# Ninety-six rows in place of 128 in the expert passes of a hybrid decoder trunk

## The chip, the core and the metric

The kernel runs on one core of a Trainium2 chip. The metric is the device time of one execution in microseconds (us). PE is the tensor engine, PEld its loads of the stationary operand, DVE, ACT and POOL are the vector, scalar and general engines, SP issues DMAs.

## What is computed

A trunk of two layers over 256 tokens of width 1024, in fp32. Each layer is a mixer (attention, short convolution, gated linear attention) and then a channel mixer: dense SwiGLU in layer 0, eight experts of which each token uses two in layer 1. The second is what the change is about:

```python
D_MODEL, SEQ, N_EXPERTS, TOP_K, D_FF_EXPERT = 1024, 256, 8, 2, 3584

def swiglu(h, wg, wu, wd):
    return (jax.nn.silu(h @ wg) * (h @ wu)) @ wd

def moe_swiglu(h, router, eg, eu, ed):
    b, s, d = h.shape
    t = h.reshape(b * s, d)
    logits = (t @ router).astype(jnp.float32)
    top_v, top_i = lax.top_k(logits, TOP_K)
    top_w = jax.nn.softmax(top_v, axis=-1)
    combine = jnp.sum(jax.nn.one_hot(top_i, N_EXPERTS, dtype=jnp.float32) * top_w[..., None], axis=1)
    out = jnp.zeros((b * s, d), jnp.float32)
    for e in range(N_EXPERTS):
        out = out + combine[:, e:e + 1] * swiglu(t, eg[e], eu[e], ed[e]).astype(jnp.float32)
    return out.astype(h.dtype).reshape(b, s, d)
```

With the inputs of the reference its router gives the eight experts 58, 51, 66, 62, 68, 69, 59 and 79 tokens (512 in all).

## The kernel before

**Precision.** Every product is made of three matmuls in fp32r (`PASSES`): high part by high part, low part of the activations by high part of the weights, high part of the activations by low part of the weights.

**Weights as a stream.** All weights come as 400 units of 128x2048 fp32 (1 MB each). SP loads them in order into six buffers `raw` (`load_unit`, L312; it waits until DVE is done with the unit six before). ACT rounds a unit into its high part `w_hi` (`hi_unit`, L327), DVE subtracts that from `raw` and so gets the low part `w_lo` (`lo_unit`, L332), PE uses both. There are three buffers of each part (`SPLIT`), so ACT waits until PE is done with the unit three before (`unit_used`). A unit feeds 12 matmuls with 512 moving columns.

**One expert.** An expert works on up to 128 of its tokens, gathered as the columns of `xT_hi` and `xT_lo`. Its 3584 hidden columns are cut into 14 blocks of 256, of three units each: two for gate and up (`gate_up`, 24 matmuls, L1828) and one for down (`down`, `down_tile`, 12 matmuls, L1852). The tokens are always the stationary operand, 128 columns wide, and the weights move past them. Between gate_up and down of a block ACT takes silu (`gate_x`, L663), DVE multiplies (`act_x`, L1141), PE transposes the block by two transposes (`act_T`, L1844), ACT copies these out as `aT_hi` (L520) and DVE subtracts to get `aT_lo` (L1167). Blocks go in pairs (`expert`): transposes of the last pair, 48 matmuls of gate_up for the next pair, 24 of down for the last. The code is written out by hand for each engine; the order on each is fixed, and semaphores join them.

**Between experts.** POOL gathers the next expert's tokens from HBM with an indirect DMA into `small`, PE transposes them with eight transposes (`gather_T`, L1977), and ACT and DVE make the two parts (`gather_hi` L520, `gather_lo` L1196). An expert's output `y_sb` goes to `outs` in HBM and is added in four pieces in the last expert (`combine`, L1184). The first expert's tokens come by matmuls (`first_tokens`, L1807).

**Too many tokens.** While the first expert runs, DVE finds out which experts have over 128 tokens (`weights` sets `flag`, `crowded` counts and lists them, L1348 to L1355), between two units of the stream. If there are any, a general loop after the end (up to three laps) runs each of these experts again on its remaining tokens. Without them the loop is skipped.

Of the kernel before, what the change touches and what calls it, by code (L numbers as in the profile page):

```python
# [16 lines left out]
F32 = mybir.dt.float32  # L17
F32R = mybir.dt.float32r
I32 = mybir.dt.int32
# [26 lines left out]
FB = 256  # L46

# [33 lines left out]
ROWS = N_EXP * P  # L81
NO_ROW = (N_EXP - 1) * P
# [37 lines left out]
def build(nc, x, stream, w_z, w_gate, conv_w, gla_gain, gains, router, gain_t, consts, masks, out):  # L120
    with ExitStack() as ctx:
# [53 lines left out]
        zero8 = sb("zero8", [P, 8])  # L175
        over_f = sb("over_f", [P, 4])
        over_i = sb("over_i", [P, 4], I32)
# [75 lines left out]
        flag = small[:, 124:132]  # L253
        cum = small[:, 132:140]
        sel = small[:, 140:148]
# [94 lines left out]
        def _(sp):  # L350
# [26 lines left out]
            n_over = sp.value_load(over_i[0:1, 0:1], min_val=0, max_val=3)  # L377
# [14 lines left out]
            with sp.If(n_over > 0):  # L392
                with sp.Fori(0, n_over) as k:
                    e = sp.value_load(over_i[0:1, bass.ds(k + 1, 1)], min_val=0, max_val=N_EXP - 1)
# [16 lines left out]
        def _(pool):  # L411
# [8 lines left out]
            nc.gpsimd.memset(zero8[:, :], 0.0)  # L420
# [60 lines left out]
            pool.dma_start(outs[NO_ROW:ROWS, :], nothing).then_inc(none_out, 16)  # L481
            def gather(e):

                pool.wait_ge(id_cp, e)
                if e == 1:
                    pool.wait_ge(tok_out, 16 * TT)
                else:
                    pool.wait_ge(gaT_ps, 2 * e)
                pool.indirect_dma_start(small[:, D:2 * D], None, tokens[:, :],
                                        bass.IndirectOffsetOnAxis(ap=tok_i[:, e:e + 1], axis=0)).then_inc(ga_in, 16)  # L490

            for e in range(N_EXP - 1):
                gather(e + 1)
                pool.wait_ge(y_done, e + 1)
                pool.dma_start(outs[e * P:(e + 1) * P, :], y_sb).then_inc(y_out, 16)
# [14 lines left out]
        def _(act):  # L510
# [144 lines left out]
            def ffn_block(S, tiles, B, par, n, d=0):  # L655

                for t in range(tiles):
# [5 lines left out]
                    nc.scalar.activation(gate_x[:, s, :], ps[:, 4 + s, 0:FB], ACT.Silu,  # L663
# [15 lines left out]
            def ffn_aT(S, tiles, B, par):  # L679
# [4 lines left out]
                else:  # L684
                    copy(aT_hi[:, par, :, :], ps[:, 6 + par, 0:FB].rearrange("p (f q) -> p f q", f=2)).then_inc(S.aT_hi, 1)

            def gathered(k):

                act.wait_ge(ga_ps, k + 1)
                copy(gath[:, 0, :], ps[:, 2, :]).then_inc(ga_act, 1)  # L690

            def gather_hi(e, q, bank=2):

                for g in range(2):
                    act.wait_ge(gaT_ps, e * 2 + (g + 1))
                    copy(xT_hi[:, 4 * g:4 * g + 4, q * P:(q + 1) * P],
                         ps[:, bank + g, :].rearrange("p (k s) -> p k s", k=4)).then_inc(ga_hi, 1)

            def y_copy(e, n, d):
# [4 lines left out]
                copy(y_sb, ps[:, 0:2, :].rearrange("p a d -> p (a d)")).then_inc(y_done, 1)  # L704

            def expert_out(k, n, d):
# [3 lines left out]
                copy(ys_hi[:, :], ps[:, 0:2, :].rearrange("p a d -> p (a d)"), w_slot[:, 0:1]).then_inc(y_hi, 1)  # L710
# [97 lines left out]
            n_over = act.value_load(over_i[0:1, 0:1], min_val=0, max_val=3)  # L808
# [3 lines left out]
            copy(ys_hi[:, 0:512], ps[:, 0, :], w_slot[:, 0:1]).then_inc(end_hi, 1)  # L812
            used(act, ALL_UNITS)
            copy(ys_hi[:, 512:D], ps[:, 1, :], w_slot[:, 0:1]).then_inc(y_hi, 1)
# [26 lines left out]
        def _(dve):  # L841
# [291 lines left out]
            def ffn_block(S, tiles, B, par, n, d=0):  # L1133

                for t in range(tiles):
# [4 lines left out]
                    else:  # L1140
                        nc.vector.tensor_tensor(act_x[:, s, :], gate_x[:, s, :], ps[:, 4 + s, FB:2 * FB], ALU.mult).then_inc(S.mul, 1)  # L1141
# [16 lines left out]
            def ffn_aT(S, tiles, B, par):  # L1158
# [5 lines left out]
                else:  # L1164
                    dst, hi = aT_lo[:, par, :, :], aT_hi[:, par, :, :]
                    src = ps[:, 6 + par, 0:FB].rearrange("p (f q) -> p f q", f=2)
                nc.vector.tensor_tensor(dst, src, hi.bitcast(F32), ALU.subtract).then_inc(S.aT_lo, 1)  # L1167

            def dispatch(e, over):

                for t in range(TT):
                    s = slot[:, t, e:e + 1] if isinstance(e, int) else slot[:, t, bass.ds(e, 1)]
                    ins = nc.vector.tensor_scalar(disp[:, t, :], iota, 128.0 if over else 0.0, s, ALU.add, ALU.is_equal)
# [13 lines left out]
            def gathered(k):  # L1187

                dve.wait_ge(ga_ps, k + 1)
                nc.vector.tensor_copy(gath[:, 1, :], ps[:, 3, :]).then_inc(ga_dve, 1)  # L1190

            def gather_lo(e, q, halves=(0, 1), bank=2):

                for g in halves:
                    dve.wait_ge(ga_hi, e * 2 + (g + 1))
                    nc.vector.tensor_tensor(xT_lo[:, 4 * g:4 * g + 4, q * P:(q + 1) * P],  # L1196
                                            ps[:, bank + g, :].rearrange("p (k s) -> p k s", k=4),
                                            xT_hi[:, 4 * g:4 * g + 4, q * P:(q + 1) * P].bitcast(F32),
# [11 lines left out]
            def expert_out(k):  # L1210

                dve.wait_ge(y_hi, k + 2)
                nc.vector.scalar_tensor_tensor(out=ys_lo[:, :], in0=ps[:, 0:2, :].rearrange("p a d -> p (a d)"),
                                               scalar=w_slot[:, 0:1], in1=ys_hi[:, :].bitcast(F32), op0=ALU.mult,
# [115 lines left out]
            def weights():  # L1330

                dve.wait_ge(total_ps, 1)
                nc.vector.tensor_scalar(flag[:, :], ps[:, 7, 16:24], float(P), None, ALU.is_gt)
# [12 lines left out]
            def crowded():  # L1346

                link(nc.vector.tensor_tensor_scan(cum[:, :], flag[:, :], zero8[:, :], 0.0, ALU.add, ALU.add))  # L1348
                link(nc.vector.tensor_copy(over_f[:, 0:1], cum[:, 7:8]))
                for k in range(3):  # L1350
                    link(nc.vector.scalar_tensor_tensor(out=sel[:, :], in0=cum[:, :], scalar=float(k + 1), in1=flag[:, :],
                                                        op0=ALU.is_equal, op1=ALU.mult))
                    link(nc.vector.tensor_tensor_reduce(out=sel[:, :], in0=sel[:, :], in1=iota8, scale=1.0, scalar=0.0,
                                                        op0=ALU.mult, op1=ALU.add, accum_out=over_f[:, k + 1:k + 2]))
                nc.vector.tensor_copy(over_i[:, :], over_f[:, :]).then_inc(route_done, 1)  # L1355

            def rows():

                link(nc.vector.scalar_tensor_tensor(out=row8[:, :, :], in0=iota8.unsqueeze(1).to_broadcast([P, TT, 8]), scalar=float(P),
# [797 lines left out]
```

## Time and profile before

| | |
|---|---|
| device time, median of 3 runs | 1416.88 us (1416.75 to 1418.26) |
| profiled execution, first to last instruction | span 1415.5 us; the page gives no other time of it |
| busy share of the span | PE 99%, PEld 82%, DVE 81%, ACT 67%, POOL 6% |
| stretch of the eight experts | from 450 us to 1403 us |
| DMA | 438 MB, 310 GB/s over the span |

The times of the three runs are of other executions than the profiled one; their median lies 1.4 us over its span. Busy PE time counts overlapping instructions once and its ends are modelled, so the distance between the starts of matmuls says more about their cost than their duration does. The rows are in a section of their own below.

### The profile page before, as it was taken

To read this page: it belongs to the slowest core of one execution; us is meant where nothing else is said; L and a number is where in the kernel's file an instruction comes from. 1 tells how busy PE (TensorE), PEld (TensorE's weight loads), DVE (VectorE), ACT (ScalarE), POOL (GpSimd) and SP (SyncE) were. 2 spreads that over 40 slices of the span, in tenths; PEclk is the share of its full clock that TensorE was granted. 3 is DMA by queue.
4 is the path that set the end of the run, shared out by engine and by line. 5 is a ranking of instruction groups with operands and counts; after the bars stand their busy time and mean duration, and the time that the engine had idled before them with its cause. 6 is when DMAs were issued, how large, how long until landed. Compare 5 with 4: busy or idle time off the path is not lost.

```text
span 1415.5 us, 18473 instructions
## 1 busy us (share of the span) xinstructions
PE 1397.5 (99%) x6936; PEld 1160.4 (82%) x6937; DVE 1147.9 (81%) x1061; ACT 945.4 (67%) x880; POOL 85.3 (6%) x65
## 2 busy tenths in 40 slices
PE   8999999999999999999999999999999999999997
PEld 6898888887988888888888888888888888888885
DVE  5766645566576989988998998988899899898997
ACT  4645444345646777777777777777777777777775
POOL 2140000001132000000000000000000000000200
PEclk9999999999999999999999999999999999999998
DMA  9434555552444999999999999999999999999992
GB/s 351 162 120 181 208 181 200 183 208 91 148 164 179 361 386 364 387 386 368 383 390 373 375 392 385 361 374 393 370 382 390 373 380 388 389 356 376 421 387 116
DMA packets 63184, 438.20 MB, mean 310 GB/s; under 512 B 7199, under 2 KB 7377, under 8 KB 11906
## 3 DMA queue, kind: packets, MB, share of 16 engines
q1 hardware_dynamic: 58896, 423.20, 78.1%
q0 software_dynamic: 4064, 13.84, 2.5%
q8 instruction: 55, 0.90, 0.3%
q14 instruction: 23, 0.19, 0.0%
q10 hardware_dynamic: 146, 0.07, 0.0%
HBM read 430.79 MB, written 6.29 MB: 309 GB/s over the span
## 4 chain that ended last, share of the span: by engine, by line
PE 96%; DVE 3%; ACT 1%; issue 0%; DMA 0%; DVEq 0%; ACTq 0%
PE ps L1828 50%; PE ps L1852 26%; PE ps L1516 4%; PE ps L1531 3%; PE ps L1619 3%; PE ps L1844 2%; PE ps L1493 2%; PE ps L1888 1%; DVE w_lo L332 1%; PE ps L1608 1%; PE ps L1553 0%; PE ps L1977 0%; PE ps L1563 0%; ACT w_hi L327 0%; PE ps L1474 0%
## 5 line engine op out<-in xcount | busy, mean ns | idle before, releaser
L332 DVE TENSOR_TENSOR w_lo<-raw,w_hi 128x2048 fp32r<-128x2048 f32 x397 | 913.8, 2304 | 173.7 <-ACT w_hi L327 172.0
L327 ACT ACTIVATE w_hi<-raw 128x2048 fp32r<-128x2048 f32 x399 | 764.0, 1915 | 211.6 <-PE ps L1852 109.1
L1828 PE MATMUL ps<-w_hi,xT_hi 128*128 128x512 f32 x1040 | 411.1, 395 | 0.5 <-DVE xT_lo L1196 0.5
L1828 PE MATMUL ps<-w_lo,xT_hi 128*128 128x512 f32 x1040 | 405.5, 390 | 0.0
L1828 PE MATMUL ps<-w_hi,xT_lo 128*128 128x512 f32 x1040 | 404.8, 389 | 0.0
L1828 PEld LDWEIGHTS ps<-w_lo,xT_hi 128*128 128x128 f32 x1040 | 195.2, 188 | 41.6
L1828 PEld LDWEIGHTS ps<-w_hi,xT_hi 128*128 128x128 f32 x1040 | 195.4, 188 | 39.8 <-DVE xT_lo L1196 0.7
L1828 PEld LDWEIGHTS ps<-w_hi,xT_lo 128*128 128x128 f32 x1040 | 195.5, 188 | 38.8
L1852 PE MATMUL ps<-w_hi,aT_hi 128*128 128x512 f32 x524 | 205.9, 393 | 0.0
L1852 PE MATMUL ps<-w_lo,aT_hi 128*128 128x512 f32 x524 | 204.4, 390 | 0.0
L1852 PE MATMUL ps<-w_hi,aT_lo 128*128 128x512 f32 x524 | 204.0, 389 | 0.0
L1852 PEld LDWEIGHTS ps<-w_hi,aT_hi 128*128 128x128 f32 x524 | 98.4, 188 | 21.0 <-DVE w_lo L332 1.2
L1852 PEld LDWEIGHTS ps<-w_lo,aT_hi 128*128 128x128 f32 x524 | 98.3, 188 | 20.8
L1852 PEld LDWEIGHTS ps<-w_hi,aT_lo 128*128 128x128 f32 x524 | 98.5, 188 | 19.9
L663 ACT ACTIVATE gate_x<-ps 128x256 f32<-128x256 f32 x112 | 43.1, 385 | 80.5 <-PE ps L1828 80.5
L520 ACT ACTIVATE aT_hi<-ps 128x256 fp32r<-128x256 f32 (+1 forms) x122 | 42.0, 392 | 38.5 <-PE ps L1844 38.5
L1167 DVE TENSOR_TENSOR aT_lo<-ps,aT_hi 128x256 fp32r<-128x256 f32 (+1 forms) x122 | 48.9, 438 | 18.1 <-ACT aT_hi L520 18.1
L1141 DVE TENSOR_TENSOR act_x<-gate_x,ps 128x256 f32<-128x256 f32 x112 | 46.4, 414 | 0.0
L1844 PEld LDWEIGHTS ps<-cst,act_x 128*128 128x128 f32 x264 | 32.9, 140 | 8.8
L1844 PE MATMUL ps<-cst,act_x 128*128 128x128 f32 x264 | 39.7, 272 | 0.0
L1516 PE MATMUL ps<-w_hi,xT_hi 128*128 128x512 f32 x96 | 38.6, 402 | 0.2
L1531 PE MATMUL ps<-xT_hi,w_hi 128*128 128x256 f32 x128 | 38.5, 301 | 0.0
(307 smaller groups left out, 1112.6 us busy)
## 6 DMA issues: line engine op xcount, KB each, us to landing
raw<-in_stream SPq DMA_DIRECT2D x400, 1024.0 KB, 7.2
outs<-work POOLq DMA_DIRECT2D x7, 512.0 KB, 9.1
gain<-in_gains POOLq DMA_DIRECT2D x4, 512.0 KB, 5.3
h<-in_x SPq DMA_DIRECT2D x2, 512.0 KB, 6.6
raw<-in_stream SPq DMA_DIRECT2D x2, 512.0 KB, 6.1
tokens<-big POOLq DMA_DIRECT2D x2, 512.0 KB, 3.8
out<-work SPq DMA_DIRECT2D x4, 256.0 KB, 2.6
cst<-in_consts SPq DMA_DIRECT2D x1, 581.0 KB, 12.2
```

Of the source, the lines that this page charges most:

```text
L327: nc.scalar.activation(home(n, 0), raw[:, n % RAW, :], ACT.Copy).then_inc(hi_done, 1)
L332: nc.vector.tensor_tensor(home(n, 1), raw[:, n % RAW, :], home(n, 0).bitcast(F32), ALU.subtract).then_inc(lo_done, 1)
L520: return nc.scalar.activation(dst, src, ACT.Copy, scale=scale)
L663: nc.scalar.activation(gate_x[:, s, :], ps[:, 4 + s, 0:FB], ACT.Silu, scale=rs[:, t:t + 1] if tiles == 2 else 1.0).then_inc(S.silu, 1)
L1141: nc.vector.tensor_tensor(act_x[:, s, :], gate_x[:, s, :], ps[:, 4 + s, FB:2 * FB], ALU.mult).then_inc(S.mul, 1)
L1167: nc.vector.tensor_tensor(dst, src, hi.bitcast(F32), ALU.subtract).then_inc(S.aT_lo, 1)
L1516: last = nc.tensor.matmul(ps[:, bank + t, :], (xT_hi, xT_lo)[xp][:, k, t * P:(t + 1) * P], w(n, wp, kk * 512, (kk + 1) * 512), start=(k == ...
L1531: last = nc.tensor.matmul(ps[:, bank + f // 2, f % 2 * SEQ:(f % 2 + 1) * SEQ], w(n, wp, kk * 512 + f * P, kk * 512 + (f + 1) * P), (xT_hi, ...
L1619: last = nc.tensor.matmul(ps[:, 2 * t + half, :], (mixT_hi, mixT_lo)[xp][:, k, t * P:(t + 1) * P], w(n, wp, kk * D + half * 512, kk * D + ...
L1828: last = nc.tensor.matmul(ps[:, 4 + s, :], (xT_hi, xT_lo)[xp][:, k, x * P:(x + 1) * P], w((n + half), wp, kk * 512, (kk + 1) * 512), start ...
L1844: last = nc.tensor.transpose(ps[:, 6 + par, c:c + P], act_x[:, s, f * P:(f + 1) * P], ident)
L1852: last = nc.tensor.matmul(ps[:, 2 * t + half, :], (a_hi, a_lo)[xp][:, f, :], w(n, wp, f * D + half * 512, f * D + (half + 1) * 512), start ...
```

## The change

An expert's pass holds `CAP` = 96 tokens. All stationary operands of its matmuls are 96 columns wide and write 96 partitions, its transposes take 96 partitions in and give 96 columns out, and the copies and DMAs around them are cut to 96. The general loop now takes the tokens over 96 in pieces of 96, so an expert can need two more pieces and there can be five in all; finding them takes a table of 16 flags in place of eight.

```diff
+CAP = 96
+MOST_OVER = 5
...
-                pool.indirect_dma_start(small[:, D:2 * D], None, tokens[:, :],
-                                        bass.IndirectOffsetOnAxis(ap=tok_i[:, e:e + 1], axis=0)).then_inc(ga_in, 16)
+                pool.indirect_dma_start(small[0:CAP, D:2 * D], None, tokens[:, :],
+                                        bass.IndirectOffsetOnAxis(ap=tok_i[0:CAP, e:e + 1], axis=0)).then_inc(ga_in, 16)
...
-                    copy(aT_hi[:, par, :, :], ps[:, 6 + par, 0:FB].rearrange("p (f q) -> p f q", f=2)).then_inc(S.aT_hi, 1)
+                    copy(aT_hi[:, par, :, 0:CAP], ps[:, 6 + par, 0:2 * CAP].rearrange("p (f q) -> p f q", f=2)).then_inc(S.aT_hi, 1)
...
-                nc.vector.tensor_scalar(flag[:, :], ps[:, 7, 16:24], float(P), None, ALU.is_gt)
+                for level in range(2):
+                    nc.vector.tensor_scalar(flag[:, level * N_EXP:(level + 1) * N_EXP], ps[:, 7, 16:24],
+                                            float((level + 1) * CAP), None, ALU.is_gt)
...
             def crowded():
 
-                link(nc.vector.tensor_tensor_scan(cum[:, :], flag[:, :], zero8[:, :], 0.0, ALU.add, ALU.add))
-                link(nc.vector.tensor_copy(over_f[:, 0:1], cum[:, 7:8]))
-                for k in range(3):
+                for level in range(2):
+                    nc.vector.tensor_scalar(later[:, :, level * N_EXP:(level + 1) * N_EXP], slot[:, :, :],
+                                            -float((level + 1) * CAP), None, ALU.add)
+                link(nc.vector.tensor_tensor_scan(cum[:, :], flag[:, :], zero16[:, :], 0.0, ALU.add, ALU.add))
+                link(nc.vector.tensor_copy(over_f[:, 0:1], cum[:, 15:16]))
+                for k in range(MOST_OVER):
...
+                pieces = over_f[:, 1:MOST_OVER + 1]
+                link(nc.vector.tensor_scalar(second, pieces, float(N_EXP), None, ALU.is_ge))
+                link(nc.vector.scalar_tensor_tensor(out=over_f[:, MOST_OVER + 1:2 * MOST_OVER + 1], in0=second,
+                                                    scalar=-float(N_EXP), in1=pieces, op0=ALU.mult, op1=ALU.add))
...
+                m = P if tiles == 2 else CAP
...
-                                last = nc.tensor.matmul(ps[:, 4 + s, :], (xT_hi, xT_lo)[xp][:, k, x * P:(x + 1) * P],
+                                last = nc.tensor.matmul(ps[0:m, 4 + s, :], (xT_hi, xT_lo)[xp][:, k, x * P:x * P + m],
...
+                            last = nc.tensor.transpose(ps[:, 6 + par, f * CAP:(f + 1) * CAP], act_x[0:CAP, s, f * P:(f + 1) * P],
+                                                       ident[0:CAP, 0:CAP])
...
-                            last = nc.tensor.matmul(ps[:, 2 * t + half, :], (a_hi, a_lo)[xp][:, f, :],
+                            last = nc.tensor.matmul(ps[0:m, 2 * t + half, :], (a_hi, a_lo)[xp][:, f, 0:m],
...
-                        last = nc.tensor.transpose(ps[:, 2 + half, kk * P:(kk + 1) * P], gath[:, half, kk * P:(kk + 1) * P],
-                                                   ident)
+                        last = nc.tensor.transpose(ps[:, 2 + half, kk * P:kk * P + CAP], gath[0:CAP, half, kk * P:(kk + 1) * P],
+                                                   ident[0:CAP, 0:CAP])
```

The order of the work changes at one place: on DVE in the first expert, between two pairs of units of the stream. Before (L1348 to L1355 are `crowded`, ISA rows the sums over the flags):

```order
L332 TENSOR_TENSOR w_lo<-raw,w_hi 128x2048 x2
L1141 TENSOR_TENSOR act_x<-gate_x,ps 128x256
L1348 SCALAR_TENSOR_TENSOR small<-small,zero 128x8
L1349 COPY over_f<-small 128x1
L1351 SCALAR_TENSOR_TENSOR small<-small 128x8
L1353 ISA small,over_f<-small,cst 128x8
L1353 ISA over_f 128x1
...
L1355 CAST over_i<-over_f 128x4
L332 TENSOR_TENSOR w_lo<-raw,w_hi 128x2048 x3
```

The three rows of L1351 and L1353 come three times. With the change (its own line numbers, five higher for act_x, nine to fifteen for `crowded`):

```order
L336 TENSOR_TENSOR w_lo<-raw,w_hi 128x2048 x2
L1146 TENSOR_TENSOR act_x<-gate_x,ps 96x256
L1357 TENSOR_SCALAR small<-small 128x2x8 x2
L1359 SCALAR_TENSOR_TENSOR small<-small,zero 128x16
L1360 COPY over_f<-small 128x1
L1362 SCALAR_TENSOR_TENSOR small<-small 128x16
L1364 ISA small,over_f<-small,cst 128x16
L1364 ISA over_f 128x1
...
L1367 TENSOR_SCALAR small<-over_f 128x5
L1368 SCALAR_TENSOR_TENSOR over_f<-small,over_f 128x5
L1370 CAST over_i<-over_f 128x11
L336 TENSOR_TENSOR w_lo<-raw,w_hi 128x2048 x3
```

The group of three now comes five times, two operations stand ahead of the scan and two behind the groups; the three units behind move by these.

On PE the order stays, and only widths change. This is the end of a pair's down, the transposes of the next act_T and the start of gate_up, before (stationary columns and moving columns for a product, partitions and columns written for a transpose):

```order
L1852 MATMUL ps<-w_hi,aT_hi 128x512
L1852 MATMUL ps<-w_hi,aT_lo 128x512
L1852 MATMUL ps<-w_lo,aT_hi 128x512
L1844 MATMUL ps<-cst,act_x 128x128 x4
L1828 MATMUL ps<-w_hi,xT_hi 128x512
L1828 MATMUL ps<-w_hi,xT_lo 128x512
```

And with the change:

```order
L1872 MATMUL ps<-w_hi,aT_hi 96x512
L1872 MATMUL ps<-w_hi,aT_lo 96x512
L1872 MATMUL ps<-w_lo,aT_hi 96x512
L1863 MATMUL ps<-cst,act_x 128x96 x4
L1844 MATMUL ps<-w_hi,xT_hi 96x512
L1844 MATMUL ps<-w_hi,xT_lo 96x512
```

The number of moving columns falls from 128 to 96 in the transposes and stays 512 in the products. In a transpose `act_x` is the stationary operand and the identity in `cst` moves past it.

## Rows read from the trace of the kernel before

**Rows 1.** Stretches: length, engines busy (instructions), granted clock, DMA share, GB/s.

```profile
500.00:700.00 200.00, 200.00 (x919) 165.83 (x917) 179.59 (x127) 150.10 (x123) 4.72 (x3) 1.00 0.98 378
1310.00:1350.00 40.00, 40.00 (x187) 33.14 (x186) 36.52 (x26) 29.36 (x25) 8.49 (x4) 1.00 1.01 421
```

**Rows 2.** Groups by line, 500 to 1300 us: busy us, mean ns, idle before.

```profile
L332 DVE TENSOR_TENSOR w_lo<-raw,w_hi 128x2048 fp32r<-128x2048 f32 x283 | 649.0, 2293 | 80.9 <-ACT w_hi L327 79.9
L327 ACT ACTIVATE w_hi<-raw 128x2048 fp32r<-128x2048 f32 x283 | 542.4, 1917 | 128.5 <-PE ps L1852 69.7 <-PE ps L1828 58.8
```

**Rows 3.** Chain that ended last: start, length, what; one pair, one gather_T.

```profile
524.00 0.87 PE ps L1977 x8
...
920.92 0.44 PE ps L1844 x4
921.36 10.91 PE ps L1828 x48
932.26 5.45 PE ps L1852 x24
```

**Rows 4.** PE timeline: start, length; 512 moving, 128 stationary columns.

```profile
907.15 0.39 PE L1828 MATMUL ps<-w_hi,xT_hi 128*128 128x512 f32 x1
...
911.91 0.39 PE L1828 MATMUL ps<-w_hi,xT_hi 128*128 128x512 f32 x1
```

**Rows 5.** PE timeline: 256 moving, 32 or 16 stationary columns, in turn.

```profile
26.18 0.28 PE L1505 MATMUL ps<-xT_lo,wz_hl 128*16 128x256 f32 x1
...
27.54 0.28 PE L1505 MATMUL ps<-xT_lo,wz_hl 128*16 128x256 f32 x1
```

**Rows 6.** PE timeline: 256 moving, 128 stationary columns.

```profile
53.55 0.28 PE L1531 MATMUL ps<-xT_hi,w_hi 128*128 128x256 f32 x1
...
55.95 0.28 PE L1531 MATMUL ps<-xT_hi,w_lo 128*128 128x256 f32 x1
```

**Rows 7.** PE timeline: plain fp32, 256 moving, 128 stationary columns.

```profile
45.80 0.59 PE L1676 MATMUL ps<-cst,work 128*128 128x256 f32 x2
```

**Rows 8.** Groups of loads by line: products, 32 stationary columns, transposes.

```profile
L1852 PEld LDWEIGHTS ps<-w_hi,aT_lo 128*128 128x128 f32 x524 | 98.5, 188 | 19.9
L1504 PEld LDWEIGHTS ps<-xT_hi,wz_hl 128*32 128x32 f32 x16 | 1.7, 108 | 0.4
L1844 PEld LDWEIGHTS ps<-cst,act_x 128*128 128x128 f32 x264 | 32.9, 140 | 8.8
```

**Rows 9.** Groups on PE: the transposes, plain fp32 with 256 and 128 columns.

```profile
L1844 PE MATMUL ps<-cst,act_x 128*128 128x128 f32 x264 | 39.7, 272 | 0.0
L1676 PE MATMUL ps<-cst,work 128*128 128x256 f32 x4 | 1.2, 378 | 0.0
L1677 PE MATMUL ps<-cst,work 128*128 128x128 f32 x4 | 0.8, 274 | 0.0
```

**Rows 10.** One line on PE, plain fp32, 64 columns: ns min/median/max.

```profile
L1573 PE MATMUL ps<-big,small x32: 221/247/275, 63.1 to 388.3; 128*128 128x64 f32 x32
```

**Rows 11.** PE and PEld timelines around one act_T.

```profile
903.97 0.60 PE L1844 MATMUL ps<-cst,act_x 128*128 128x128 f32 x4
...
904.30 0.19 PEld L1828 LDWEIGHTS ps<-w_hi,xT_hi 128*128 128x128 f32 x1
904.41 0.19 PEld L1828 LDWEIGHTS ps<-w_hi,xT_lo 128*128 128x128 f32 x1
```

**Rows 12.** DVE timeline in the first expert: start, length.

```profile
474.67 0.17 DVE L1348 TENSOR_TENSOR_SCAN small<-small,zero 128x8 f32<-128x8 f32 x1
...
475.06 0.17 DVE L1351 SCALAR_TENSOR_TENSOR small<-small 128x8 f32<-128x8 f32 x1
...
475.47 0.17 DVE L1351 SCALAR_TENSOR_TENSOR small<-small 128x8 f32<-128x8 f32 x1
...
476.37 2.28 DVE L332 TENSOR_TENSOR w_lo<-raw,w_hi 128x2048 fp32r<-128x2048 f32 x1
```

**Rows 13.** PEld timeline there: start, length, idle before.

```profile
478.71 0.19 PEld L1828 LDWEIGHTS ps<-w_hi,xT_hi 128*128 128x128 f32 x1 [0.26 <-DVE w_lo L332]
```

## What the change will do: the prediction

> **What bounds the kernel now.** I read the stretches first. While the experts run PE is busy all the time, with its clock granted in full (1.00, the 2.4 GHz level), DVE for 90% and ACT for 75% [rows 1]. Then the chain of waits: a pair of blocks is 4 transposes, 48 and 24 matmuls, 16.80 us together, with no other engine in it [rows 3]. The 56 pairs of eight experts are about 941 us of the 1415.5 us span. So a change counts where it shortens what PE does, or where it makes PE wait.
>
> Who comes next? DVE has six units of 2293 ns in a pair [rows 2], 13.8 us, and its small copies; it waits for ACT, and ACT waits for PE (128.5 us of ACT's idle time [rows 2]). Both follow PE. The DMA engines show a share of 0.98 at 378 GB/s, but when the last gathers are added they move 421 GB/s and PE stays busy [rows 1]; a pair that is 0.1 us (0.6%) shorter asks for some 380, so DMA still follows too.
>
> **The products: 4032 matmuls, taken as unchanged.** The experts have 112 blocks of 24 and 12 matmuls. Their stationary operand goes from 128 to 96 columns, and 512 columns move as before. From 907.15 to 911.91 are 21 matmuls: 226.7 ns each, or 0.443 ns per moving column [rows 4]. Twelve matmuls with 256 moving columns and only 32 or 16 stationary ones take 1.36 us, 113.3 ns each: again 0.443 ns per column [rows 5]. The time is proportional to the moving columns alone, and these do not change. The load of the stationary operand does get shorter: 188 ns for 128 columns and 108 for 32 [rows 8], 0.83 ns per column, so some 161 ns for 96. But it runs beside the matmul before, whose 226.7 ns cover it. The cost of a shorter load is nothing here; if it lay bare, 27 ns would count 4032 times.
>
> By the Trainium skill, "TensorE: Matmul & The Clock Gate", section "Packing small matmuls — row/col tiling", a load overlaps matmuls in flight only when its row group differs. All these loads use the same rows, so by that rule load and matmul would stand in line. The same page's section "LDWEIGHTS (loading the stationary operand)" puts 128 columns at 107 ns; matmul and load would then be over 300 ns apart, and the sum would gain 4032 x 26.7 ns = 108 us. The trace disagrees: starts are 226.7 ns apart, and a load of 188 ns fits within that.
>
> Bounds for this term: nothing at one end. At the other, matmuls with 256 moving and 128 stationary columns come every 120 ns (20 of them in 2.40 us [rows 6]), 6.7 ns more than the narrow ones. If that difference belongs to the width (some 104 columns), 32 columns are 2.1 ns, and 4032 of them 8.3 us. I take nothing: at 256 columns the load is about as long as the matmul and may itself set 120 ns, and plain fp32 with 128 stationary columns comes every 0.59 - 0.378 = 0.21 us [rows 7, 9], hardly more than two cycles (0.83 ns) for each of 256 columns, which leaves no room for a large cost of width.
>
> **The transposes: 5.8 us less.** Here the moving operand is the identity, and it falls from 128 to 96 columns. Four take 0.44 us and eight 0.87 us, 109 ns each [rows 3]. Is that the moving side? Plain fp32 matmuls last 221 ns at best for 64 columns [rows 10], 274 for 128 and 378 for 256, and a transpose 272 [rows 9]: 0.82 ns per column, and the transpose lies on the same line. Its load is no obstacle as I read it: it lasts 140 ns where that of a product lasts 188 [rows 8], so its part that can't overlap is some 48 ns shorter. 32 columns fewer are then 26.7 ns per transpose, 82 ns in place of 109. The last of each group gains nothing: the load of the next product begins with it (904.30) and the product's own successor is loaded at 904.41, 0.11 us later [rows 11]; that load keeps nearly its length. So a group of four gains 3 x 26.7 = 0.080 us, and there are 55 of them and two of two: 4.5 us. A group of eight gains 0.187 us, seven times: 1.3 us. Sum 5.8 us. Bounds: nothing, if the load of 128 columns (of `act_x`, not narrowed) sets 109 ns; 7.5 us if all 280 gain.
>
> **The five pieces: 1.45 us more.** `crowded` takes 476.37 - 474.67 = 1.70 us of DVE [rows 12], and behind it are three units. PE needs the first of them right away: it waits for it, with an idle load queue of 0.26 us [rows 13]. So what DVE does longer here PE waits longer. Two more groups cost 2 x 0.41 us (475.06 to 475.47); the two operations behind them 0.2 us each, as the first two (0.39 us for both); the two ahead, which don't wait for each other, 0.1 to 0.2 us each [rows 12]. That is 1.4 to 1.6 us; I take 1.45. Later units have room: three units of 2.29 us [rows 2] meet a PE that takes 2.72 us for each (12 x 226.7 ns), so DVE catches up, but what PE lost stays lost. One more flag operation comes earlier, beside an idle wait; nothing.
>
> **What else changes, at nothing.** Copies out of PSUM get up to a quarter fewer columns (aT, xT), or fewer partitions at the same length (act_x, gate_x, y). All lie on ACT and DVE, under PE. The DMAs for gathers and outputs shrink from 128 to 96 rows, beside the stream. In the last expert four additions to the residual (`combine`) lie on DVE between units; a pair's transposes stand ahead of the place where these could set the pace, so their gain stands. At the end the last matmuls and copies keep their lengths.
>
> **Sum.** -5.8 + 1.45 = -4.3 us against the profiled execution (span 1415.5 us). Its span lies 1.4 us below the median of the runs; put on the median the forecast is 1416.9 - 4.3 = 1412.6 us, 0.30% less. About 0.2% (2.8 us) is what a measurement of this kernel can tell from no change.
>
> **Rivals.**
> - *The load sets the transposes.* For: their stationary operand stays 128 columns, and 109 ns is close to what 128 columns at 0.83 ns give (107). Against: the shorter load row of 140 ns and the common line of 221, 272 and 378. Then only `crowded` is left: +1.45 us, 1418.3 us. Chance 0.24.
> - *The width of the stationary operand counts in products too.* For: 120 against 113.3 ns. Against: equal ns per column at 256 and 512. Then 8.3 us more are gained: 1404.3 us. Chance 0.08.
> - *A 96-row transpose loses the short load, and the kernel gets slower.* Place: the same 280 transposes. If their load becomes as long as a product's, the row nearest is the 120 ns of rows 6, where load and matmul are alike: (120 - 109) x 280 = +3.1 us, with `crowded` +4.5 us, 1421.4 us. It decides from 114 ns per transpose on, (2.8 - 1.45) us / 280. For: no row shows a transpose with anything but 128 rows and columns. Chance 0.08.
> - *Loads stand in line with matmuls.* Against it stand the starts and the length of a load [rows 4, 8]; if 27 ns were gained in each product, 1305 us. Chance 0.01.
> - *An expert has over 96 tokens.* Then the general loop runs: at least seven pairs of 16.8 us, 118 us more, 1530 us. The counts given with the reference end at 79. Chance 0.01.
>
> In the Trainium skill, "TensorEngine Tiling (Array Packing)", "Restrictions" says that column tiling switches the fp32 transpose mode off; by its list of modes (64 or 32 columns) 96 is not tiled, and no run here shows it.
>
> **Range and chances.** The forecast holds with 0.58; its own range is 1410.8 (all transposes gain, cheap `crowded`) to 1414. To get 8 in 10 I add the rival without a gain, up to 1419 with a dear `crowded`, and a little below for a width that counts in part: 1409.5 to 1419.0. The two slow ends and the wider gains stay outside. Faster by over 0.2%: the forecast but for its dear edge (0.55), width (0.08) and 0.01: 0.64. Slower: 0.09 (0.08 and 0.01). The same: 0.27.
>
> **What would show it.** Transposes in the chain: 4 in about 0.35 to 0.36 us, 8 in 0.68, as against 0.44 and 0.87. Products still 226.7 ns apart, loads 161 ns. A pair 16.72 us. The idle load ahead of the product behind `crowded` grows from 0.26 to about 1.8 us. Wrong would be: products below 226 ns, transposes still at 109 or above, or DVE or a DMA named in waits of PE where there are none now.

## The result, and the profile after

| | before | after |
|---|---|---|
| device time, median of 8 runs | 1417.26 us (1416.75 to 1418.66) | 1421.38 us (1420.96 to 1422.39) |
| span of the profiled execution | 1415.5 us | 1420.5 us |

The change makes the kernel 0.27% slower: ratio 1.0027, 95% interval 1.0018 to 1.0036, or 4.1 us. The forecast was 4.3 us less. One of the four runs of the last kernel below (before, with narrow products) took 1748.95 us at a mean granted clock of 0.753, where the other three have 0.996 to 0.998, and stands outside of its median.

The stretches of after, with the columns of [rows 1]:

```profile
500.00:700.00 200.00, 200.00 (x913) 141.68 (x912) 177.03 (x127) 147.93 (x123) 2.50 (x3) 1.00 0.98 377
1310.00:1350.00 40.00, 40.00 (x184) 28.36 (x183) 36.12 (x26) 29.26 (x24) 10.36 (x4) 1.00 1.01 412
```

PE is still busy all the time at the granted clock of 1.00, and the DMA share is the same. But from 500 to 1300 us it gets through 3653 instructions (913 of them in the row above) where it had 3668, though some of them, the transposes, should have become cheaper. Nothing else got slower: DVE and ACT are busy for less, and DVE idles more behind ACT, ACT more behind PE. The groups of after by line from 500 to 1300 us (columns as in [rows 2]):

```profile
L336 DVE TENSOR_TENSOR w_lo<-raw,w_hi 128x2048 fp32r<-128x2048 f32 x282 | 646.4, 2292 | 91.5 <-ACT w_hi L331 91.4
L331 ACT ACTIVATE w_hi<-raw 128x2048 fp32r<-128x2048 f32 x282 | 540.0, 1915 | 132.7 <-PE ps L1872 71.2 <-PE ps L1844 60.9
```

The idle times of both rose (80.9 to 91.5 us, 128.5 to 132.7 us [rows 2]), and what they wait for at the root is PE. So the time is lost on PE itself, and it must be looked for in its own instructions. The chain of waits of after (start, length, what), a pair and one `gather_T`:

```profile
526.29 0.66 PE ps L1997 x8
...
924.48 0.33 PE ps L1863 x4
924.81 11.05 PE ps L1844 x48
935.86 5.52 PE ps L1872 x24
```

The transposes went the forecast way and a little further, 0.44 to 0.33 us for four and 0.87 to 0.66 for eight [rows 3]. The products went the other way: 48 of gate_up from 10.91 to 11.05 us, 24 of down from 5.45 to 5.52 [rows 3]. A pair is 16.90 us, where it was 16.80. The PE timeline shows it for each one:

```profile
924.89 0.39 PE L1844 MATMUL ps<-w_hi,xT_lo 128*96 128x512 f32 x1
...
926.96 0.39 PE L1844 MATMUL ps<-w_hi,xT_lo 128*96 128x512 f32 x1
```

From the first start to the tenth are nine steps in 2.07 us: **230.0 ns each, where 128 stationary columns gave 226.7** [rows 4]. The duration of one reads 0.39 us in both. Only the distance of the starts shows the 3.3 ns. By that times 4032 the products would cost 13.3 us; this is an upper value, as the last experiment shows.

The loads, in one line's instructions (ns min/median/max, first and last start), and a timeline of PEld behind the counting of `crowded`:

```profile
L1844 PEld LDWEIGHTS ps<-w_hi,xT_lo x1040: 161/161/192, 143.4 to 1395.4; 128*96 128x96 f32 x150, 128*128 128x128 f32 x24
L1863 PEld LDWEIGHTS ps<-cst,act_x x224: 137/141/143, 464.4 to 1401.9; 96*128 96x128 f32 x112
```

```profile
480.78 0.16 PEld L1844 LDWEIGHTS ps<-w_hi,xT_hi 128*96 128x96 f32 x1 [1.68 <-DVE w_lo L336]
```

A load of 96 columns takes 161 ns, as forecast. The idle load queue grew from 0.26 us [rows 13] to 1.68 us.

**Where the 5.0 us between the spans lie.** The distances between the groups of transposes in the two chains give it piece by piece. The profiled execution of after is the longest of its eight (1422.39 us), 1.0 us over their median. Ahead of the experts' first group 0.6 us differ; 60 narrower products are 0.2 of it, and the rest is in work that the change doesn't touch. The first two pairs take 32.77 us in place of 31.18 (`crowded`): +1.6. An ordinary expert of seven pairs takes 119.4 us in place of 119.0: +0.1 in each of five pairs, less where `gather_T` lies; six experts make +2.4, and the rest of the first one +0.4. The end of the last expert, from the transposes at 1328.30 us (1333.39 in after) to the last ones, takes 68.7 us in place of 69.0: -0.3. Together +4.1 us. The other 0.3 us lie behind the last transposes.

### The profile page after: what moved, and what is told of

It is laid out like the page before. It is cut to its first block, busy times and chain, and to the rows that moved or that the text cites. A ratio compares the mean times of both kernels' runs of the same rounds, so it can differ in the third digit from the quotient of the medians.

```text
span 1420.5 us, 18484 instructions
## 1 busy us (share of the span) xinstructions
PE 1401.1 (99%) x6936; PEld 1049.2 (74%) x6937; DVE 1139.4 (80%) x1072; ACT 937.6 (66%) x880; POOL 84.6 (6%) x65
## 4 chain that ended last, share of the span: by engine, by line
PE 95%; DVE 3%; ACT 1%; issue 0%; DMA 0%; DVEq 0%; ACTq 0%
PE ps L1844 50%; PE ps L1872 25%; PE ps L1531 4%; PE ps L1546 3%; PE ps L1634 3%; PE ps L1508 2%; PE ps L1863 1%; DVE w_lo L336 1%; PE ps L1908 1%; PE ps L1623 1%; ACT w_hi L331 1%; PE ps L1568 0%; PE ps L1578 0%; PE ps L1489 0%; PE ps L1997 0%
## 5 line engine op out<-in xcount | busy, mean ns | idle before, releaser
L1844 PE MATMUL ps<-w_hi,xT_hi 128*96 128x512 f32 (+1 forms) x1040 | 411.3, 395 | 1.8 <-DVE w_lo L336 1.5
L1844 PE MATMUL ps<-w_lo,xT_hi 128*96 128x512 f32 (+1 forms) x1040 | 407.2, 392 | 0.0
L1844 PE MATMUL ps<-w_hi,xT_lo 128*96 128x512 f32 (+1 forms) x1040 | 407.0, 391 | 0.0
L1844 PEld LDWEIGHTS ps<-w_hi,xT_lo 128*96 128x96 f32 (+1 forms) x1040 | 171.7, 165 | 63.2
L1872 PE MATMUL ps<-w_hi,aT_hi 128*96 128x512 f32 (+1 forms) x524 | 206.3, 394 | 0.0
L1872 PE MATMUL ps<-w_lo,aT_hi 128*96 128x512 f32 (+1 forms) x524 | 205.2, 392 | 0.0
L1872 PE MATMUL ps<-w_hi,aT_lo 128*96 128x512 f32 (+1 forms) x524 | 205.0, 391 | 0.0
L1531 PE MATMUL ps<-w_hi,xT_hi 128*128 128x512 f32 x96 | 38.5, 402 | 0.3
L1531 PE MATMUL ps<-w_lo,xT_hi 128*128 128x512 f32 x96 | 37.5, 391 | 0.0
L1531 PE MATMUL ps<-w_hi,xT_lo 128*128 128x512 f32 x96 | 37.4, 390 | 0.0
```

What stands on the lines that cost most here:

```text
L1531: last = nc.tensor.matmul(ps[:, bank + t, :], (xT_hi, xT_lo)[xp][:, k, t * P:(t + 1) * P], w(n, wp, kk * 512, (kk + 1) * 512), start=(k == ...
L1844: last = nc.tensor.matmul(ps[0:m, 4 + s, :], (xT_hi, xT_lo)[xp][:, k, x * P:x * P + m], w((n + half), wp, kk * 512, (kk + 1) * 512), start ...
L1872: last = nc.tensor.matmul(ps[0:m, 2 * t + half, :], (a_hi, a_lo)[xp][:, f, 0:m], w(n, wp, f * D + half * 512, f * D + (half + 1) * 512), s ...
```

## The experiments

Two accounts stand against each other. **A: the width.** A product with fewer than 128 stationary columns is itself about 3.3 ns longer, wherever it stands; narrower transposes gain, `crowded` costs what was forecast. **B: what came with the width.** The product is the same, and something around it slows it: shorter transposes, narrower accesses of DVE and ACT, the units that `crowded` shifted. Where an expectation words a rival more closely, that wording holds. All kernels but the last were made from the changed one. The code of each is cut; "..." marks what is left out. With each the time of before on the same chip is given. Batches are 1417.79 us (16 runs), 1418.16 (9) and 1417.53 (7).

**Products 128 wide again, all else narrow.**

```diff
+WIDE = 128
...
-                m = P if tiles == 2 else CAP
+                m = P if tiles == 2 else WIDE
...
-                    last = down_tile(n, t, aT_hi[:, s], aT_lo[:, s], first, final, m=P if tiles == 2 else CAP)
+                    last = down_tile(n, t, aT_hi[:, s], aT_lo[:, s], first, final, m=P if tiles == 2 else WIDE)
...
```

The last expert's end is changed in the same way. The columns from 96 on hold what earlier work left there, and nobody reads what comes of them.

> Edit: the change, but the stationary operands of the experts' products (gate_up, down, expert_end) stay 128 columns wide; transposes, copies, DMAs and crowded as in the change. Theory A (the width of the stationary operand costs 3.3 ns in each product): products come every 226.7 to 227 ns again, a pair takes 16.80 - 0.11 = 16.69 us, and the time is 4032 x 3.3 ns = 13 us under the change: about 1408 to 1410 us. Theory B (products are slower for another cause, such as the narrower copies and reads of PSUM beside them): still 230 ns, time as with the change, 1421 us.

1413.64 us (7 runs), before 1417.79: ratio 0.9972, 0.996 to 0.9983. Its chain of waits:

```profile
919.79 10.95 PE ps L1845 x48
930.75 5.44 PE ps L1873 x24
936.19 0.33 PE ps L1864 x4
```

24 products of down are back at 5.44 us, 226.7 ns each, with the 96-wide transposes, copies and the longer `crowded` all in place. With the width back the kernel is 4.2 us faster than before, nearly the forecast's sum of -4.3. The time that A had expected, 1408 to 1410 us, was missed all the same: it is 7.7 us under the change and not 13. A pair is 16.73 us, 0.07 less than before. In the chain four transposes gain 0.11 us and 48 products lose 0.04 of it; the starts say where (means over 47 groups of transposes between 500 and 1300 us). From a group's first transpose to the first product are 277 ns in place of 355, which is three times 26. From the first product to the second are 314 ns, as in before (315), and the nine steps after that have 231.3 ns each in place of 230.0. So with 128-wide products three of four transposes gain, as the prediction had it.

**Other widths.** The same edit with WIDE = 112, 64, 120, 80 and 32. With 64 and 32 the products of some tokens are left out; the instructions and their order stay.

> Edit: the change with 112 wide products (columns 96 to 111 are stale and their results not used). Theory A1: between, some 228.3 ns. Theory A2 (a cost by whole quarters of 32): 112 is in the fourth quarter, 226.7 ns. Theory B: 230 ns.

> Edit: the change with 64 wide products; rows 64 to 95 of each expert's products are left out (what is read there is stale). Theory A1 (the cost grows as the operand gets narrower): over 230 ns, some 233. Theory A2 (only a width of three quarters costs, two, one and four do not): 226.7 ns. Theory B: 230 ns as with the change.

> Edit: the change with 120 wide products (columns 96 to 119 stale, not used). 112 gave 229.2 ns, 96 and 64 gave 230.0, 128 gives 226.7. If the cost follows the length of the load (shorter by 0.83 ns per column), 120 lies between: 228 ns, pairs 16.78 us. If it is a yes or no of full width with 112 as noise, 230 ns, pairs 16.9 us.

> Edit: the change with 80 wide products (rows 80 to 95 left out, no expert has so many tokens). 112 gave 229.2 ns and 120 gave 233.3, so odd widths can cost more than 96. If multiples of 32 cost 3.3 ns and others other amounts: anything but 230.0 ns. If 3.3 ns is the cost of every width that is a multiple of 16: 230.0 ns.

> Edit: the change with 32 wide products (rows 32 to 95 of each expert's products are left out). 96 and 64 gave 230.0 ns, and 256 moving columns by 96 gave 116.7 ns where 32 and 16 wide ones had 113.3. If every width under 128 costs 3.3 ns: 230.0 ns. If 32 is a width without it, as the rows at 113.3 ns suggest: 226.7 ns, pairs of about 16.66 us.

| stationary columns | 24 of down, us | spacing, ns | load, ns | pair, us | time of one run, us |
|---|---|---|---|---|---|
| 128 | 5.44 | 226.7 | 188 | 16.73 | 1413.64 (median) |
| 120 | 5.60 | 233.3 | 181 | 17.14 | 1434.71 |
| 112 | 5.50 | 229.2 | 174 | 16.84 | 1419.68 |
| 96 (the change) | 5.52 | 230.0 | 161 | 16.90 | 1421.38 (median) |
| 80 | 5.60 | 233.3 | 148 | 17.11 | 1433.47 |
| 64 | 5.52 | 230.0 | 134 | 16.90 | 1420.54 |
| 32 | 5.56 | 231.5 | 109 | 17.01 | 1427.05 |

The chain of waits with 120 columns, then with 32:

```profile
930.45 11.21 PE ps L1845 x48
941.66 5.60 PE ps L1873 x24
```

```profile
927.23 11.11 PE ps L1845 x48
938.34 5.56 PE ps L1873 x24
```

Every width under 128 is slower than 128, and there is no slope in it: eight columns fewer cost most, as much as 48 fewer and twice as much as 32 fewer. The load shortens evenly (0.82 ns per column), so its length alone doesn't set the time. The expectations did badly here. At 64 both forms of A were out, and the 230 ns of B came true although the kernel above had spoken against B; 112 lay between the values named, 120 and 32 beside them; for 80 only the alternative that named no value came true, and 32 then broke its premise of 3.3 ns for every multiple of 32. After 112 and 64 a step to one fixed value had looked right, and there is none. One run of each is enough for the spacing, since it is the mean of thousands of steps in one trace. The single steps aren't alike: at 96 they go from 228 to 232 ns, at 80 from 229 to 238, at 64 from 224 to 236, over and over, while at 128 nearly all are 226 or 227 once a stream runs.

**`crowded` in eight pieces** over the pairs of experts 1 and 2, with 96-wide products; and with 128-wide ones.

```diff
-                    if isinstance(e, int) and e == 0 and p == 0:
-                        crowded()
+                    if isinstance(e, int) and e in (1, 2) and p < 5:
+                        next(counting, None)
...
+                yield
...
+                yield
                 for k in range(MOST_OVER):
...
+                    yield
...
+            counting = crowded()
```

> Edit: the change with 96 wide products, but crowded is cut into eight steps of at most 0.6 us that stand in eight pairs of experts 1 and 2, in place of one burst in expert 0. If the burst is PE's wait of 1.5 us there, it goes: 1.5 to 1.7 us less than the change, about 1419.7 us, and no idle load over 0.3 us behind expert 0's first pair. If that wait only hides another one (a unit that is late anyway), PE waits elsewhere and the time stays at 1421.4 us.

> Edit: both remedies at once on the change: products 128 wide, crowded in eight steps over experts 1 and 2. If the two costs are separate they add: the time of wide_128 (1413.6 us) less the 1.7 us that spread_96 gained, about 1411.9 us, 0.4% under the kernel before; pairs 16.73 us, expert 0's first two pairs 30.9 us. If PE, once faster, meets another wait there, 1413 us or more.

1419.59 us (10 runs; ratio 1.0015, 1.0006 to 1.0025), 1.8 us under after, and 1412.64 us (5 runs; ratio 0.9964, 0.995 to 0.9977). Chain of the first, in the first expert:

```profile
477.97 0.33 PE ps L1868 x4
478.31 11.05 PE ps L1849 x48
489.35 5.52 PE ps L1877 x24
```

Behind the transposes the products follow at once; the wait for `w_lo` (1.68 us in after) is gone, and the first two pairs take 31.04 us in place of 32.77. The 1.73 us are the whole of `crowded` on the path; before it cost 0.26 of them. The products stay at 230.0 ns, so the shifted units had no part in it. In the second kernel the first two pairs take 30.74 us where the one with `crowded` in one piece takes 32.55; the medians differ by 1.0 us across the batches, and by 1.4 us with each set against the before of its batch. 1411.9 us and 30.9 us had been expected.

**Eighty tokens in a pass,** products 128 wide, `crowded` spread.

```diff
-CAP = 96
+CAP = 80
```

> Edit: spread_128 with 80 tokens in place of 96 in an expert's pass (no expert has over 79 here; the general loop of this kernel would not cover over 160 for one expert). If a transpose costs by its moving columns, 0.83 ns each, 13.3 ns less for all but the last of each group: 3 x 56 and 7 x 7 of them, 2.9 us less than spread_128, pairs 16.69 us, four transposes 0.28 us. If the load of 128 columns (0.8 x 128 = 107 ns less what overlaps) already sets 82 ns, no gain at all and four stay at 0.33 us.

1409.52 us (1408.67 to 1410.05; ratio 0.9939, 0.9926 to 0.9953), 3.1 us under the same with 96. Its chain:

```profile
928.35 5.44 PE ps L1878 x24
933.80 0.28 PE ps L1869 x4
```

Four transposes of 80 moving columns take 0.28 us, 70 ns each; 96 take 82 and 128 took 109 [rows 3]. So each moving column fewer saves some 0.82 ns, and the load of 128 columns (141 ns above) sets nothing down to 80. This is the fastest of the kernels that compute everything. But it isn't general: a pass and the two pieces that its table has room for serve an expert up to 240 tokens (not 160, as the expectation says), and 256 can come.

**256 moving columns,** 96 stationary, in gate_up. The up half of gate_up is left out.

```diff
-                                last = nc.tensor.matmul(ps[0:m, 4 + s, :], (xT_hi, xT_lo)[xp][:, k, x * P:x * P + m],
-                                                        w((n + half), wp, kk * 512, (kk + 1) * 512),
+                                last = nc.tensor.matmul(ps[0:m, 4 + s, 0:512 if tiles == 2 else 256], (xT_hi, xT_lo)[xp][:, k, x * P:x * P + m],
+                                                        w((n + half), wp, kk * 512, kk * 512 + (512 if tiles == 2 else 256)),
```

> Edit: the change with only 256 of the 512 moving columns in gate_up (the up half is left out, what is read of it is stale), stationary 96 wide. If narrow products lose a fixed 3.3 ns each, 113.3 + 3.3 = 116.6 ns between starts; if they lose by moving column, 115.0 ns; if the loss is only there where a load is much shorter than its matmul, 113.3 ns as with 16 and 32 columns before. The whole time says nothing, DVE then sets the pace.

The PE timeline of it:

```profile
904.96 0.28 PE L1844 MATMUL ps<-w_hi,xT_lo 128*96 128x256 f32 x1
...
906.13 0.28 PE L1844 MATMUL ps<-w_lo,xT_hi 128*96 128x256 f32 x1
```

Ten steps in 1.17 us are 117 ns (single steps have 112 to 121); half of 226.7 is 113.3. Against that half the extra is again some 3.3 ns, which would be a fixed amount per matmul and not a share of its columns. That is not shown: no kernel has 128 stationary columns at 256 moving ones in this place, and the one row that has them elsewhere, [rows 6], has 120 ns. Against that row the narrow ones are the faster. The kernel takes 1350.81 us; PE now waits for `w_lo` in each block, and the bound has moved to DVE, so its time says nothing of the width.

**96 of 128 rows of the contraction** in gate_up, all 128 columns. A quarter of each sum is left out.

```diff
+                rows_in = P if tiles == 2 else 96
...
-                                last = nc.tensor.matmul(ps[0:m, 4 + s, :], (xT_hi, xT_lo)[xp][:, k, x * P:x * P + m],
-                                                        w((n + half), wp, kk * 512, (kk + 1) * 512),
+                                last = nc.tensor.matmul(ps[0:m, 4 + s, :], (xT_hi, xT_lo)[xp][0:rows_in, k, x * P:x * P + m],
+                                                        w((n + half), wp, kk * 512, (kk + 1) * 512)[0:rows_in],
```

> Edit: the kernel of wide_128 with only 96 of the 128 rows (contraction) in gate_up's products; a quarter of each contraction is left out. If any operand that does not fill the array costs 3.3 ns: gate_up at 230 ns. If only the number of stationary columns matters: 226.7 ns as in wide_128, and pairs of 16.73 us.

```profile
936.81 10.96 PE ps L1846 x48
```

The chain has 10.96 us for 48, the same as the 128-wide kernel, and the one run took 1413.87 us. Fewer rows cost these products nothing; it is the columns of the stationary operand that count. The 24 products of down behind them, with all 128 rows, take 5.47 us in place of 5.44. Nothing here says why.

**The kernel before, with its products 96 wide and nothing else.**

```diff
+                m = P if tiles == 2 else 96
...
-                                last = nc.tensor.matmul(ps[:, 4 + s, :], (xT_hi, xT_lo)[xp][:, k, x * P:(x + 1) * P],
+                                last = nc.tensor.matmul(ps[0:m, 4 + s, :], (xT_hi, xT_lo)[xp][:, k, x * P:x * P + m],
```

(and the same in down and at the last expert's end)

> Edit: the kernel before, and of the change only the 96 wide stationary operands of gate_up, down and expert_end (no expert has over 96 tokens here); transposes, copies, DMAs and crowded stay as before. If the width alone costs 3.3 ns per product at any surroundings: 230.0 ns between starts, a pair 16.80 + 72 x 0.0033 = 17.04 us less 0.03 for the shorter first load, 4032 x 3.3 ns = 13 us less 2 us over the kernel before, about 1428 to 1430 us. If the cost needs the change's narrow transposes or copies beside it: 226.7 ns and 1417 us.

1428.04 us (median of 3), before 1417.53: ratio 1.0069, 1.0049 to 1.009. The chain:

```profile
927.11 11.04 PE ps L1829 x48
938.15 5.52 PE ps L1853 x24
943.67 0.44 PE ps L1845 x4
```

Here the copies, the transposes (0.44 us) and `crowded` are those of before, and the products still take 230.0 ns. Account B falls. **The width alone costs 10.5 us** (7 to 13 by the interval); between the first and the last group of transposes in the experts the two traces differ by 9.5 us. That is less than 4032 x 3.3 ns = 13.3 us, and the starts say why. Two of before, not far ahead of [rows 4]:

```profile
904.86 0.39 PE L1828 MATMUL ps<-w_lo,xT_hi 128*128 128x512 f32 x1
...
906.48 0.39 PE L1828 MATMUL ps<-w_hi,xT_hi 128*128 128x512 f32 x1
```

These seven steps take 1.62 us, 231 ns each: behind a group of transposes the 128-wide stream doesn't have its 226.7 ns yet. On the mean over 47 groups the nine steps after the second product are 230.0 ns in before and 229.9 in the narrow kernel. So some ten of 48 steps have no extra, 0.03 us per pair and nearly 2 us in all. In the last expert the longer products take the place of waits, as the next section shows (0.7 us). Some 0.5 to 1 us is not placed.

## Why the prediction was wrong, step by step

*What bounds the kernel:* right. PE is busy throughout before and after, and every change of a pair came from PE's own instructions.

*The products, "taken as unchanged":* this is the step that failed. "The time is proportional to the moving columns alone" doesn't hold: 230.0 ns with 96 stationary columns, 226.7 with 128. Two pairs of rows had been made to carry it. The first [rows 5] had 32 and 16 stationary columns in turn at 256 moving and 113.3 ns; here a stream of 32-wide ones at 512 has 231.5, more than twice 113.3 (226.7), and 96 at 256 has 117. So those rows don't speak for a stream of one narrow width. The second [rows 6] has 120 ns for 128 columns at 256, which was read as width; but 128 is the fastest width at 512, so that isn't it either. The bounds were nothing and 8.3 us of gain, and no bound on the side of a loss was set, although no row showed 96 columns. This left the loss that came, 0.0033 us times 4032 at most, outside of the sum. With 4032 instructions, 0.7 ns on each is already the 2.8 us that count as measurable. The argument that a load that isn't bare costs nothing holds as far as it goes: the load is 161 ns as said, beside a matmul of 230.

*The transposes, 5.8 us less:* mechanism right, size a little small. Each is 26.5 ns shorter, and in the change all of them gain, close to the upper bound given, 280 x 26.5 = 7.4 us. The gain of the last of a group shows between the first product and the second, 291 ns in place of 315. It takes a narrow transpose and a narrow load behind it: with only one of the two (the 128-wide kernel, before with narrow products) it stays at 314 and 315 ns. So "the last of each group gains nothing" was sound for a load that "keeps nearly its length"; but the prediction had itself put that load at 161 ns in place of 188.

*The five pieces, +1.45 us:* right. The first two pairs took 1.59 us longer with two groups of transposes 0.2 us shorter and 132 slower products in them (+0.4); spreading took 1.73 us out where before waits 0.26. The idle load went to 1.68 us, 1.8 had been said.

*Everything else, at nothing:* right for the pairs; no copy, DMA or wait of another engine shows in them. In the last expert DVE adds the outputs to `h`, and PE waits for it a little. The waits of PEld from 1333 to 1400 us (engine, line, waited for: us in total, times, longest), after:

```profile
PEld ps L1872 <- DVE w_lo L336: 0.9, 3, 0.3
```

and the 128-wide kernel:

```profile
PEld ps L1873 <- DVE w_lo L337: 1.1, 3, 0.4
```

It was 1.2 us in before and 0.6 in before with narrow products: slower products eat a part of the wait up. "Their gain stands" holds. From the transposes at 1328.30 us of before (their like in the others) to the last ones before takes 69.01 us and the 128-wide kernel 68.62, before with narrow products 69.14 and after 68.67: narrow transposes save 0.4 to 0.5 us in both. What is smaller there is the loss by the products: 0.13 us, where four ordinary pairs lose 0.8.

*The sum:* -4.3 was forecast, and with the products' width taken back the kernel measures -4.2 (2.4 to 5.7 less by its interval). The width alone measures +10.5. Added, that is +6.3, and the change measures +4.1. The medians carry an uncertainty of some microseconds into such a sum. Between the first and the last group of transposes in the experts the traces give -3.7, +9.5 and +4.1 us, so the two help each other by 1.7 us. Of this 55 x 24 ns = 1.3 us are the step from the first product to the second, which shortens only where both are narrow; the rest is about what the 128-wide kernel loses in the nine steps behind it (55 x 12 ns = 0.7 us).

*The rivals:* the one that came to 1421.4 us hit the time, and it was wrong in its mechanism: it had 96-row transposes go from 109 to 120 ns, and they went to 82. A rival with the right number is no right rival. The width as a gain in the products had the place right and the sign wrong. The load doesn't set the transposes. No load stands in line with a matmul; no expert ran over.

*The rule of the Trainium skill* ("TensorE: Matmul & The Clock Gate", section "Packing small matmuls — row/col tiling") on loads that overlap only with other row groups was weighed and refused by the rows; it stays refused. All seven widths load the same rows, and in each the load lies beside the matmul before (188 ns within 226.7, 109 within 231.5). The Trainium skill, "TensorE: Matmul & The Clock Gate", section "Back-to-back issue gap", gives the gap of isolated matmuls as the moving columns over 2.4 plus 2.5 ns, which makes an estimate of 215.8 ns for 512, and 131 ns for 512 in a stream of loads and matmuls; neither has the stationary columns in it. The fp32r products here disagree with both: 226.7 ns at best, and up to 233.3 by the width.

**What stays open.** Why a narrower stationary operand lengthens the step isn't settled. That the width does it is shown, by taking it back in the change and by putting it alone into before. The means are close to steps of 3.3 ns, eight cycles at 2.4 GHz: none at 128, one at 96 and 64, two at 120 and 80, while 112 (2.5 ns) and 32 (4.8 ns) are off them. Since the single steps differ by up to 12 ns, this may be chance. A shorter load and fewer partitions written into PSUM go with each other in every one of these kernels. Either could be the cause, and no kernel was made that parts the two. Whether anything but fp32r behaves so wasn't tried.

## What to carry over

Narrow the moving operand, and with 512 moving columns keep the stationary one at 128 even where some of its columns are empty: here the columns that aren't needed were free, and leaving them out cost 2.5 to 6.7 ns of every fp32r matmul. Measure before carrying this over to 256 moving columns: there the rows have 120 ns with 128 stationary ones [rows 6], 117 with 96 and 113.3 with 32 and 16 in turn [rows 5], each in another place. Where a kernel issues thousands of the same instruction, "unchanged" is a term with a count and needs a bound on both sides; a row with another size, in another pattern, is a bound and no proof. Here the narrow pass was worth 4.2 us (ratio 0.9972), and with its counting spread 5.5 us (ratio 0.9964), once the products were left alone.

## What had not been expected of the hardware

- The spacing of fp32r matmuls with 512 moving columns isn't monotone in the stationary columns: 226.7 ns at 128, then 233.3, 229.2, 230.0, 233.3, 230.0 and 231.5 ns at 120, 112, 96, 80, 64 and 32. Only at 128 are the single steps even, and behind a group of transposes it takes that stream some ten steps to get there.
- Fewer rows of the contraction (96 of 128) change nothing in these products (10.96 us for 48), and a plain fp32 transpose with 96 or 80 rows in costs 82 or 70 ns (109 with 128), with its load of 128 columns beside it.
- Neither the durations of single matmuls in the trace (0.39 us at either width) nor the busy share show any of this. The distance of the starts does.
